# A transformer of two blocks on one Trainium2 core: new order at the opening, at the block boundaries, in the latent stage and at the dilated tail

## What is computed

```python
for layer in range(2):                                   # first block
    h = rmsnorm(x, norm_mix_pre[layer])
    m = retention_mixer(h, ...) if layer == 0 else dilated_mixer(h, ...)
    x = x + rmsnorm(m, norm_mix_post[layer])
    f = conv_ffn(rmsnorm(x, norm_ffn_pre[layer]), ...)   # (gelu(conv(gate)) * val) @ w_down
    x = x + rmsnorm(f, norm_ffn_post[layer])
for l in range(2):                                       # second block
    h = h + hybrid_mixer(rms_norm(h, norm_mix[l]), ...)
    h = h + memory_cross_attention(rms_norm(h, norm_xattn[l]), mem, norm_mem[l], ...)
return rms_norm(h, norm_final)
```

## Time and profile before

| | us |
|---|---|
| median of 3 runs | 1282.46 (1281.28 to 1283.64) |
| the profiled execution | 1283.59 |
| its span | 1281.8 |
| PE busy | 1254.6 (98%) |
| DVE busy | 807.1 (63%) |
| ACT busy | 692.6 (54%) |
| POOL busy | 140.3 (11%) |

### The profile page before, as it was taken

The page is one execution under the profiler, slowest core; times in us unless marked ns, Lnnn a source line. Parts: engine busy times, 40 slices in busy tenths (PEclk is TensorE's granted clock), DMA queues, the critical chain, the costliest instruction groups (busy, mean ns, idle before and its releaser), DMA issues. The chain is left out here.

```text
span 1281.8 us, 19334 instructions
## 1 busy us (share of the span) xinstructions
PE 1254.6 (98%) x7584; PEld 1122.9 (88%) x7584; DVE 807.1 (63%) x1217; ACT 692.6 (54%) x979; POOL 140.3 (11%) x181
## 2 busy tenths in 40 slices
PE   8999999999999999999999999999999999999997
PEld 7888878888888999999987888888988998998996
DVE  5466656766767556666666867667555666565554
ACT  5444335655555555555545656555665556564554
POOL 0000002100001000000001211411001400101500
PEclk9999999999999999999999999999999999999999
DMA  8544443655553544444452655555353352462331
GB/s 317 200 165 164 165 158 124 250 186 178 194 187 117 197 148 148 148 149 146 139 184 78 241 192 178 193 173 182 106 189 125 131 197 99 132 212 101 132 132 50
DMA packets 33559, 208.55 MB, mean 163 GB/s; under 512 B 3953, under 2 KB 4226, under 8 KB 15938
## 3 DMA queue, kind: packets, MB, share of 16 engines
q1 hardware_dynamic: 31392, 200.36, 44.8%
q0 software_dynamic: 1488, 5.78, 1.3%
q10 hardware_dynamic: 594, 1.23, 0.3%
HBM read 206.30 MB, written 1.05 MB: 162 GB/s over the span
## 5 line engine op out<-in xcount | busy, mean ns | idle before, releaser
L1811 DVE TENSOR_TENSOR wlo<-raw,whi 128x2048 fp32r<-128x2048 f32 (+5 forms) x208 | 430.7, 2077 | 238.0 <-ACT whi L1314 237.3
L1314 ACT ACTIVATE whi<-raw 128x2048 fp32r<-128x2048 f32 (+5 forms) x208 | 361.4, 1742 | 203.5 <-PE pair L584 171.1
L670 PE MATMUL pair<-ahl,whi 128*128 128x512 f32 x672 | 238.1, 398 | 2.0 <-issue 1.4
L582 PE MATMUL pair<-whi,bhi 128*128 128x384 f32 (+3 forms) x544 | 194.7, 358 | 5.5 <-issue 3.0
L583 PE MATMUL pair<-wlo,bhi 128*128 128x384 f32 (+3 forms) x544 | 189.1, 348 | 0.0
L584 PE MATMUL pair<-whi,blo 128*128 128x384 f32 (+3 forms) x544 | 189.0, 347 | 0.0
L671 PE MATMUL pair<-ahl,wlo 128*128 128x256 f32 x672 | 188.5, 280 | 0.0
L582 PE MATMUL pair<-whi,ahl 128*128 128x384 f32 (+3 forms) x416 | 154.8, 372 | 3.2 <-DVE wlo L1811 3.2
L670 PEld LDWEIGHTS pair<-ahl,whi 128*128 128x128 f32 x672 | 126.2, 188 | 33.5 <-issue 2.9
L583 PE MATMUL pair<-wlo,ahl 128*128 128x384 f32 (+3 forms) x416 | 150.3, 361 | 0.0
L584 PE MATMUL pair<-whi,ahl 128*128 128x384 f32 (+3 forms) x416 | 149.9, 360 | 0.0
(11 more groups left out here) (305 smaller groups left out, 1910.3 us busy)
## 6 DMA issues: line engine op xcount, KB each, us to landing
raw<-wstream_d SPq DMA_DIRECT2D x136, 1024.0 KB, 4.9
raw<-wstream_d SPq DMA_DIRECT2D x56, 768.0 KB, 4.2
raw<-wstream_d SPq DMA_DIRECT2D x4, 832.0 KB, 4.4
raw<-wstream_d SPq DMA_DIRECT2D x4, 800.0 KB, 4.3
gain_row<-rows_d POOLq DMA_DIRECT2D x5, 512.0 KB, 4.0
arena<-mem_d POOLq DMA_DIRECT2D x2, 1024.0 KB, 7.8
raw<-wstream_d SPq DMA_DIRECT2D x3, 512.0 KB, 7.4
raw<-wstream_d SPq DMA_DIRECT2D x4, 384.0 KB, 3.2
```

Source lines behind the costliest of these rows:

```text
L582: pe.matmul(out_ap, lhi, rhi, start=first, stop=False, skip_group_check=True)
L670: pe.matmul(pair[:, p, f, :], whi[:, slot, sl], both, start=k == 0, stop=k == KD - 1, skip_group_check=True)
L1314: act.activation(whi[:, n % RING, 0:width[n]], raw[:, n % RAW, 0:width[n]], ACT.Copy).then_inc(hi_ready, 1)
L1811: dve.tensor_tensor(wlo[:, n % RING, 0:width[n]], raw[:, n % RAW, 0:width[n]], whi[:, n % RING, 0:width[n]].bitcast(F32), ALU.subtract).th ...
```

## The change

It touches ten places; nothing is computed differently but for the order of sums and the pieces of the post-norm.

SP: the first chunk comes in quarters; chunk 2 and then the columns and tables are issued here, no longer on ACT (with the gate and the positions, which aren't shown).

```diff
...
-FIRST_PARTS = ((0, 512, 1024, CW), (0, 1024, CW))
+FIRST_PARTS = ((0, 512, 1024, 1536, CW), (0, 1024, CW))
...
-    c = len(FIRST_PARTS)
+    for c in range(len(FIRST_PARTS), RAW):
+        load(c)
...
+    sp.dma_start(tables[:, :], ret_in).then_inc(ret_tables_in, 16)
...
+    c = RAW
...
```

```diff
-    def post_rsqrt(eps=(EPS, D * EPS)):
...
-        rsqrt(ssq_ready, w.up("ssq"), sq_sum[:, 0:1], rstd[:, 0:1], 1.0 / D, eps=eps[0])
...
-        pool.tensor_scalar(var_eps[:, 0:1], sq_sum[:, 1:2], sq_sum[:, 2:3], eps[1], ALU.add, ALU.add).then_inc(rstd_step, 1)
...
+    def post_rsqrt(eps=(D * EPS, D * EPS)):
...
+            pool.wait_ge(ssq_ready, w.up("ssq", 2))
+            pool.tensor_scalar(var_eps[:, 0:1], sq_sum[:, 2 * t:2 * t + 1], sq_sum[:, 2 * t + 1:2 * t + 2], eps[t],
+                               ALU.add, ALU.add).then_inc(rstd_step, 1)
...
```

```diff
+                if c == 0 and s == 0:
...
+                    pe.wait_ge(part_hi, 1)
+                    pe.wait_ge(turned_hi, 1)
+                    for f in range(4):
+                        pe.matmul(accs[f], whi[:, slot, f * P:(f + 1) * P], hi[:, k0, :], start=f % 2 == 0, stop=False, skip_group_check=True)
+                    lhs_ready(0, 2)
+                    for f in range(4):
+                        pe.matmul(accs[f], whi[:, slot, f * P:(f + 1) * P], lo[:, k0, :], start=False, stop=False, skip_group_check=True)
+                    pe.wait_ge(part_lo, 1)
+                    for f in range(4):
+                        pe.matmul(accs[f], wlo[:, slot, f * P:(f + 1) * P], hi[:, k0, :], start=False, stop=False, skip_group_check=True)
+                    continue
...
+        if lhs_ready is not None:
+            high_ready = w.at("turn") - KD // 2
+            for step, j in (("low", 0), ("low", 1), ("high", 0), ("low", 2), ("high", 1), ("low", 3), ("high", 2), ("high", 3)):
+                if step == "low":
+                    pe.wait_ge(turned_hi, high_ready + j + 1)
+                else:
+                    lhs_ready(2 * j, 2 * j + 2)
+                for k in (2 * j, 2 * j + 1):
+                    for f in range(2):
+                        sl = slice((2 * k + f) * P, (2 * k + f + 1) * P)
+                        if step == "low":
+                            mm = pe.matmul(pair[:, p, f, SEQ:2 * SEQ], wlo[:, slot, sl], ahi[:, k, :], start=k == 0, stop=False, skip_group_check=True)
+                        else:
...
+                            mm = pe.matmul(pair[:, p, f, :], whi[:, slot, sl], both, start=False, stop=k == KD - 1, skip_group_check=True)
+            mm.then_inc(chunk_used, 1)
+            w.chunk += 1
+            return
...
-            if lhs_ready is not None and k % 2 == 0:
-                lhs_ready(k, k + 2)
...
-    def to_model(hi, lo, tiles, first, last, into=None, between=(), tile_ready=None, second_free=None):
+    def to_model(hi, lo, tiles, first, last, into=None, between=(), tile_ready=None, second_free=None, by_tile=False):
...
         if last:
-            todo.sort(key=lambda i: (i[2], i[2] * i[1]))
+            todo.sort(key=lambda i: (i[0] if by_tile else 0, i[2], i[1]))
...
-            if last and i in (len(todo) // 2 - 1, 3 * len(todo) // 4 - 1):
+            if last and s == len(tiles) - 1 and i < len(todo) - 1:
...
-            if (i + 1) % 4 == 0 and between:
+            if (i + 1) % (2 if by_tile else 4) == 0 and between:
...
     ready = turn_rows(loaded)
+    keep_warm(pair[:, 1, 0, 0:P], 8)
...
-    into = summed_in_pairs()
+    second_free = []
+    into = summed_in_pairs(second_free)
...
     follow = {0: lambda: ret_scores(last), 1: lambda: ret_mix(last), 3: lambda: ret_turn(last)}
...
-        to_model(bhi, blo, (2 * i, 2 * i + 1), i == 0, i == RET_KT // 2 - 1, into)
+        to_model(bhi, blo, (2 * i, 2 * i + 1), i == 0, i == RET_KT // 2 - 1, into, second_free=None if i else second_free)
...
     def ffn(l):
-        ready = turn_rows(added, ((14, 5, 7) if l else (15, 6, 7)))
+        ready = turn_rows(added, (4, 9, 2))
...
                 up_tile(ready if j == 0 else None)
-                up_tile(between=() if j else [spread_rows], merged=j < UPS - 1)
+                up_tile(between=() if j else [nothing, nothing, spread_rows], merged=j < UPS - 1)
...
-    pe.wait_ge(post_ready, 1 + 3)
-    ready = turn_rows(added, (6, 0, 10), aside)
+    pe.wait_ge(post_ready, 2 + 4)
+    ready = turn_rows(added, (0, 2, 10), aside)
...
     for b in range(PAIRS):
...
-            at[3] = spread_phases
+            at[5] = spread_phases
...
     c = PAIRS - 1
-    into = summed_in_pairs()
+    second_free = []
+    into = summed_in_pairs(second_free)
...
-             nothing, lambda: dil_pturn(c, 0), lambda: (dil_pturn(c, 1), dil_mix(c))]
+             nothing, lambda: dil_pturn(c, 0), lambda: dil_pturn(c, 1), lambda: dil_mix(c)]
...
-        pe.wait_ge(o_split, 2 * (i + 1))
-        to_model(bhi, blo, (KD + 2 * i, KD + 2 * i + 1), i == 0, i == KD // 2 - 1, into, steps[2 * i:2 * i + 2])
+        at_end = i == KD // 2 - 1
+        pe.wait_ge(o_split, 2 * i + 1 if at_end else 2 * (i + 1))
+        to_model(bhi, blo, (KD + 2 * i, KD + 2 * i + 1), i == 0, at_end, into, steps[2 * i:2 * i + 2],
+                 (lambda s: pe.wait_ge(o_split, KD - 1 + s)) if at_end else None, None if i else second_free, at_end)
...
-                pe.wait_ge(post_ready, 2 * (1 + 3))
+                pe.wait_ge(post_ready, 2 * (2 + 4))
...
         def gla_turn():
...
-            pe.wait_ge(gla_dve, gd + 5)
+            pe.wait_ge(gla_dve, gd + 4)
...
         mem_pturn(2)
-        into = summed_in_pairs()
+        second_free = []
+        into = summed_in_pairs(second_free)
...
-        to_model(bhi, blo, (0, 1), True, False, into, between=[third_mix])
+        to_model(bhi, blo, (0, 1), True, False, into, between=[third_mix], second_free=second_free)
...
```

```diff
+    act.activation(warm_exp, ones, ACT.Square).then_inc(act_step, 1)
...
+                else:
...
+                act.activation(scratch[:, t, nb, :], sums[:, nb, :], ACT.Square, accum_out=sq_sum[:, i:i + 1]).then_inc(ssq_ready, 1)
...
-    first_hi(0, 0)
...
+    first_hi(0, 0)
...
+    first_rows(1)
...
-    first_rows(1)
+    first_hi(0, 3)
...
-    act.dma_start(tables[:, :], ret_in).then_inc(ret_tables_in, 16)
...
+    split_hi(-1)
...
     def ret_out(h):
...
     for h in range(RET_HEADS):
...
-        catch_up()
...
+        catch_up()
...
     def ffn(l):
...
-        row_square(0, added)
...
-        row_square(1, added)
+        row_squares(added)
...
+            if l and i == 2 * MEM_AT + 1:
+                mem_out(0, 0)
...
-                mem_out(0, 0)
...
-            if i == FF_TILES - 1 or l and i == 2 * MEM_AT + 1:
+            if i == FF_TILES - 1:
...
+                passed()
...
+                catch_up()
...
+    catch_up()
...
+            used(1)
...
-        used(2)
+        used(2 if b else 1)
...
         act.activation(g_lr[0:GLA_RANK, :], bank[0:GLA_RANK, 2, 0:SEQ], ACT.Copy).then_inc(gla_act, 1)
...
+        act.activation(warm_exp, ones, ACT.Exp).then_inc(act_step, 1)
...
```

```diff
+        def weigh(t, nb):
...
+            dve.wait_ge(ssq_ready, w.up("ssq"))
+            ins = dve.scalar_tensor_tensor(xg[:, t, nb, :], sums[t][:, nb, :], float(D) ** 0.5, gains[:, nb, :], ALU.mult, ALU.mult)
+            ins.then_inc(done[t][0] if nb else post_ready, 1)
...
-        dve.wait_ge(ssq_ready, w.up("ssq"))
-        dve.tensor_tensor(xg[:, 0, :, :], sums[0], gains, ALU.mult).then_inc(done[0][0], 1)
-        dve.wait_ge(ssq_ready, w.up("ssq"))
-        dve.scalar_tensor_tensor(xg[:, 1, 0, :], sums[1][:, 0, :], float(D) ** 0.5, gains[:, 0, :], ALU.mult, ALU.mult).then_inc(post_ready, 1)
+        weigh(0, 0)
+        weigh(0, 1)
...
-        dve.wait_ge(ssq_ready, w.up("ssq"))
-        dve.scalar_tensor_tensor(xg[:, 1, 1, :], sums[1][:, 1, :], float(D) ** 0.5, gains[:, 1, :], ALU.mult, ALU.mult).then_inc(done[1][0], 1)
...
+        weigh(1, 0)
+        weigh(1, 1)
...
+    first_rows(0)
...
-    first_rows(0)
...
+    first_rows(1)
...
-    first_rows(1)
+    first_lo(0, 3)
...
+    split_lo(-1)
...
         used(2)
...
-        used(2)
+        used(1)
+        passed()
...
+        catch_up()
...
-            if i % 2 and i > 1:
+            if l and i == 2 * MEM_AT + 1:
+                passed()
+                mem_out(0, 1)
+                catch_up()
+            elif i % 2 and i > 1:
...
-            if l and i == 2 * MEM_AT + 1:
-                mem_out(0, 1)
...
+        dve.wait_ge(drained_a[p_kr[0]], p_kr[1])
...
-        dve.wait_ge(drained_a[p_kr[0]], p_kr[1])
...
+            mla_out(g)
...
-            mla_out(g)
```

More of the change, by code:

```diff
@@ L1348, in post_squares @@
                 scratch = post_scratch[:, :, :].rearrange("p t (n c) -> p t n c", n=2)
-                act.wait_ge(half_summed, w.up("half"))
-                act.activation(scratch[:, 0, :, :], first, ACT.Square, accum_out=sq_sum[:, 0:1]).then_inc(ssq_ready, 1)
```

(16 more changed lines are left out.)

55 lines of the change are left out of this document (31 added, 24 removed).

## The result

The changed kernel takes 1260.23 us (median of 4, 1260.11 to 1260.38) against 1282.73 for the kernel before in the same comparison (1281.28 to 1283.64): 22.5 less, ratio 0.9826, 95% interval 0.9809 to 0.9843. The profiled execution took 1260.11, its span is 1258.3, 23.5 less than the span before.

The account below looks back on a forecast made before the run. TensorE (PE), busy 98% of the span, was taken as the bound, so only its waits could be won: terms summing to 19.9 us, less 1.4 for residual waits, 18.5 off the 1282.46 median, gave 1264.0, range 1261 to 1271.

Parts of the forecast that it names:

- the opening: Start of the kernel: first product at 9.0, chunk 2 split as it lands, next block at 21.9 instead of 24.9; 3.0 us.
- the boundaries: Between mixers and FFNs, post-norm in halves: retention to FFN 0 1.8, FFN 0 to dilated 1.4, dilated to FFN 1 0.3 us.
- the hole before FFN 1: Dilated to FFN 1: PE stands empty about 1.4 us once its four fillers have run.
- new low stretch ahead of the tail: Rival: the clock falls elsewhere, each drop costing 1.5; one or two give 1265.5 to 1267 us; chance 0.2.
- row chains that were not late: Rival at the post-norms and dilated tail: row chains stay late, some 4 to 5 given back, 1269 us; chance 0.12.
- chunk 2 at 15.08: Rival in the opening: chunk 2 lands 3 us later than the estimated 15, giving 1267 us; chance 0.07.
- the 0.6 of the forecast: Opening: PE was expected to wait some 0.6 us at the fifth k, as DVE's queue is no shorter.
- Memory's last chunk: Memory output: tile 1's second low part asked for one group sooner, a stall of 0.4 us against the buffer waits' gain.
- the MLA heads: MLA outputs put before the next maxima, so the wait at L1143 goes; 1.0 us.
- 0.1 at each of 14 places: Deduction over the whole sum: a removed wait seldom goes to nothing, so 1.4 us was taken off.
- buffer waits: Retention, dilated and memory outputs, with FFN 1's memory rows: six "issue" waits go, 4.4, less a stall of 0.4; 4.0 us.
- the two stretches at 0.50: Half-speed clock in the opening (26.42) and layer 1, expected to go with the waits ahead of them; 1.5 us each.

Follow-up runs that it names:

- u_second: Changed kernel with the second pair buffer waited for at once again in the retention, dilated and memory outputs; span 1262.2 us.
- u_mem: Changed kernel with FFN 1's memory rows behind the splits again, on ACT and DVE; span 1260.0 us.
- u_gla: Changed kernel with gla_turn waiting for the third factor again; span 1259.5 us.
- u_mla: Changed kernel with MLA's outputs behind the maxima again; span 1260.1 us.
- v_chunk2: Kernel before with one part of the opening alone: chunk 2 split as it lands, tables and columns issued by SP; span 1277.8 us.
- before_again: Kernel before, unchanged, profiled a second time; 1281.01 us, span 1279.2.
- u_open: Changed kernel with chunk 2 split behind the row squares again and the four DMAs back on ACT's queue; span 1261.0 us.
- u_rope: Changed kernel with DVE's k-rope behind the state scans again; span 1262.0 us.

## Why the prediction was too small

*What held.* The mechanism of every part but one, and for the opening, the boundaries and the hole before FFN 1 also the size, to 0.25. Of the rivals none came: no new low stretch ahead of the tail, row chains that were not late, chunk 2 at 15.08. The stall inside the opening prints 0.29 of idle, but by start times it is the 0.6 of the forecast: from 14.87 to 15.44 instead of 0.12, and 0.1 more at the next matmul, 0.55. Memory's last chunk lost 0.53 by the timeline instead of 0.4. The part that held by half is the MLA heads: they were to lose both waits at L1143, 1.0. Only 0.6 of that idle went, and that the place gave 1.53 all the same is luck as far as this forecast goes, as two stalls at the first heads, 0.3 each, stood in no row.

*What failed, first,* is this term of the sum: "A removed wait seldom goes to nothing ... I leave 0.1 at each of 14 places, 1.4." It had the wrong sign, since the wait itself was mis-sized: the prediction took the printed idle for its whole price. At the waits that were priced from the earlier trace rows (buffer waits, tail, table load, `gla_turn`, k-rope, MLA) the idle that went was 10.4, what came was 13.9 by the table (the memory's new stall of 0.53 taken out), and u_second, u_mem, u_gla and u_mla measured the same by putting them back: 0.95 for 0.69, 1.42 for 1.30, 0.79 for 0.54, 0.52 for 0.37, 0.34 for none. A stall is 0.1 to 0.3 dearer than the idle beside it. Idle is counted from the drawn end of the matmul before, which lies behind the usual start of the next (0.39 long at a pitch of 0.23, 0.34 at 0.19, 0.28 at 0.12). And the second matmul after a stall can start late: in the block of the earlier trace rows the first starts at 24.91 and the second at 25.25, 0.34 later instead of 0.23. Over the stalls of the kernel before this second part is 0.07 to 0.11 for products, and 0.06 or less for transposes of 128. Between 18.5 and the span's 23.5 are 5.0: 1.4 of wrong sign, 3.0 at these places, and 0.6 at the opening, the stretches and the boundaries, each a little under. The opening's 0.25 has the same cause: its wait of 2.28 gave 2.5, here and in v_chunk2.

*Second, in the other direction:* the two stretches at 0.50, 1.5 each, were taken from one profile as if the kernel always had them. That profile did, and its execution is 1.1 over the median; the second profile had none. So of 3.06 measured between two profiles only a part is in the medians, and 22.5 stands for 23.5. Between before_again and the changed kernel's profile, neither with a stretch ahead of the tail, the spans differ by 20.9; the forecast without its 3.0 for the clock is 15.5. So the rest of the sum was 5.4 short, and the clock's 3.0, counted in full, hid part of it. The kernel before gave 1280.5 to 1285.9 over all its runs in this study, the changed one 1260.0 to 1260.4. The changed kernel's times agree with each other, which fits that chances for a low stretch went with the long waits, but doesn't show it. The slowest runs of the kernel before, 3 to 4 over its median, were not profiled. Their mean granted clock is known: 0.994 in the two slowest (1285.70, 1285.85), 0.999 in two of the three quickest (1280.47, 1280.82), 0.997 in the third. An estimate from these: a mean lower by 0.005 is 0.01 more of the span at 0.50, so some 13 us, about four stretches of 3.4. At 1.5 each they cost 6 us, and the times differ by 5.2. So most of the spread looks like low stretches, but not all of it: one run took 1284.30 at 0.998.

*The range* allowed 1.5 below the full sum of 19.9, for waits not priced, and needed 2.3.

## What to carry to other kernels

Price a removed wait of a pipelined engine by start times, last start before to first start after less the usual pitch, not by the idle that the profile prints. Here the printed idle lacked 0.1 to 0.3 us each time, and stalls up to 0.3 were not printed at all. Profile a kernel twice before a stretch of low clock enters a sum: what repeats is the wait, not the stretch. And where an order hides one wait at a tail, look at once what the next stage loses: of the 2.0 that the order by tile won, 1.1 went into the hole behind it.

## What the runs showed of the hardware

- The same wait (2.28 at 24.91 in the kernel before, 2.27 at 24.42 in u_open) was followed by 3.4 us at half clock in the one and by none in the other; the kernel before itself had two such stretches in one execution and none in the next. In u_rope a wait of 0.76 in two layers was followed by a stretch in one of them.
- With filler transposes of 128 columns the clock stayed at 1.00 through 4 to 6 us of boundary in all 15 profiles; without them it was at 0.50 in three of four cases at the two later boundaries, and at 1.00 at the first.
- A POOL operation on 128x1 took 0.30 beside DVE operations with a PSUM operand, and 0.94 and 1.17 beside one that reads SBUF twice.
